# A two-block transformer kernel: in its last mixer, window scores and their softmax are placed between the two compressions

## The reference

```python
def compress(t, pos, w1, w2):
    blocks = t[:, cidx] + pos[None, None, :, None, :]
    flat = blocks.transpose(0, 3, 1, 2, 4).reshape(Bn, G, n_cmp, CMP_BLOCK * E)
    return (jax.nn.gelu(flat @ w1) @ w2).astype(f32)
...
p_c = masked_softmax(q . k_cmp + bias, dist_c >= 0);   o_c = p_c . v_cmp
p_s = masked_softmax(q . k_sel + bias, dist_s >= 0);   o_s = p_s . v_sel
p_w = masked_softmax(q . k_win + bias, valid_w);       o_w = p_w . v_win
out = g[0] * o_c + g[1] * o_s + g[2] * o_w
```

## Time and profile before

| | us |
|---|---|
| median of 3 runs | 2382.18 (2381.37 to 2387.04) |
| the profiled execution | 2387.23 |
| its span (first to last instruction) | 2385.4 |
| PE busy | 2247.4 |
| DVE busy | 1490.9 |
| ACT busy | 1084.2 |

### The profile page before, as it was taken

How to read it: one execution, slowest core, us unless ns; L and a number is a source line. 1 busy time by engine, 2 the same in 40 slices (tenths; PEclk the granted TensorE clock), 3 DMA queues, 4 the chain that set the end, 5 groups by cost and what they waited for, 6 DMA issues and landing times.

```text
span 2385.4 us, 36673 instructions
## 1 busy us (share of the span) xinstructions
PE 2247.4 (94%) x13862; PEld 1876.2 (79%) x13862; DVE 1490.9 (63%) x2345; ACT 1084.2 (45%) x1544; POOL 241.2 (10%) x241
## 2 busy tenths in 40 slices
PE   8999999999999999899999789999989788999997
PEld 6678667999767866799976679887879477988786
DVE  2946355755394635585534677888764267788876
ACT  1132452344214245244433355676654265667665
POOL 1914000101091400021100000000000000000000
PEclk9999899999999999999999989999999898999999
DMA  4332113455333212356532236888845413688884
GB/s 153 127 121 89 63 64 131 165 180 172 121 132 115 88 64 71 136 174 196 187 130 98 71 140 211 314 298 310 294 165 177 141 45 142 221 309 305 303 293 140
DMA packets 109808, 396.86 MB, mean 166 GB/s; under 512 B 12088, under 2 KB 14144, under 8 KB 109376
## 3 DMA queue, kind: packets, MB, share of 16 engines
q1 hardware_dynamic: 108576, 393.45, 48.5%
q10 hardware_dynamic: 1056, 1.06, 0.1%
HBM read 393.40 MB, written 1.06 MB: 165 GB/s over the span
## 4 chain that ended last, share of the span: by engine, by line
PE 80%; DVE 14%; ACT 4%; issue 2%; DMA 1%; DVEq 0%; SPq 0%; ACTq 0%
PE psum L541 78%; DVE W_LO L1642 3%; PE psum L549 1%; DVE region L1647 1%; DMA ring<-in_weights 1%; DVE region L1650 1%; ACT region L1218 1%; DVE RS L1679 1%; DVE X_LO L1647 1%; DVE SQ L1647 1%; ACT W_HI L1213 1%; ACT SQ L1218 0%; ACT L1218 0%; DMA PAR<-in_params 0%; ACT XT L1218 0%
## 5 line engine op out<-in xcount | busy, mean ns | idle before, releaser
L1642 DVE TENSOR_TENSOR W_LO<-ring,W_HI 128x1024 fp32r<-128x1024 f32 x434 | 531.9, 1226 | 217.6 <-ACT W_HI L1213 207.1
L1213 ACT ACTIVATE W_HI<-ring 128x1024 fp32r<-128x1024 f32 x434 | 461.1, 1062 | 330.4 <-PE psum L541 245.3
L541 PE MATMUL psum<-HN,ring 128*128 128x272 f32 (+1 forms) x1600 | 384.3, 401 | 9.7 <-DVE HN L1654 9.7
L541 PEld LDWEIGHTS psum<-HN,ring 128*128 128x128 f32 x1600 | 308.6, 195 | 78.8 <-issue 18.3
L541 PE MATMUL psum<-X_HI,W_HI 128*128 128x256 f32 x800 | 229.1, 286 | 9.3 <-DVE W_LO L1642 6.9
L541 PE MATMUL psum<-X_LO,W_HI 128*128 128x256 f32 x800 | 224.5, 281 | 0.0
L541 PE MATMUL psum<-X_HI,W_LO 128*128 128x256 f32 x800 | 224.4, 280 | 0.0
L1222 ACT ACTIVATE region<-psum 128x272 f32<-128x272 f32 (+9 forms) x227 | 89.7, 395 | 287.2 <-PE psum L541 270.8
L1642 DVE TENSOR_TENSOR W_LO<-SQ,W_HI 128x1024 fp32r<-128x1024 f32 x128 | 156.9, 1226 | 37.1 <-ACT W_HI L1213 32.8
L541 PE MATMUL psum<-FN_HI,W_HI 128*128 128x272 f32 (+1 forms) x592 | 169.2, 286 | 0.0
L541 PE MATMUL psum<-W_HI,XG_HI 128*128 128x512 f32 x384 | 152.9, 398 | 17.3 <-DVE W_LO L1642 15.3
(11 more groups left out here) (323 smaller groups left out, 4268.4 us busy)
## 6 DMA issues: line engine op xcount, KB each, us to landing
ring<-in_weights SPq DMA_DIRECT2D x615, 512.0 KB, 4.2
SQ<-in_weights SPq DMA_DIRECT2D x128, 512.0 KB, 4.8
XT<-in_x SPq DMA_DIRECT2D x1, 1088.0 KB, 5.1
CST<-in_consts SPq DMA_DIRECT2D x1, 1082.5 KB, 7.3
SQ<-bias_by_distance ACTq DMA_DIRECT2D x1, 1024.0 KB, 5.8
out<-XT SPq DMA_DIRECT2D x8, 128.0 KB, 1.9
PAR<-in_params SPq DMA_DIRECT2D x1, 572.0 KB, 8.2
bias_by_distance<-MIX ACTq DMA_DIRECT2D x1, 12.0 KB
```

The lines of the kernel that those rows point to most:

```text
L541: ins = nc.tensor.matmul(dst, w, x, start=start, stop=stop, skip_group_check=True)
L1213: lane(nc.scalar.activation(W_HI[:, s % SPLIT, :], ring_slot(n), ACT.Copy), split_hi)
L1642: lane(nc.vector.tensor_tensor(W_LO[:, s % SPLIT, :], ring_slot(n), W_HI[:, s % SPLIT, :].bitcast(F32), ALU.subtract), split_lo)
```

## The change

`BLK` becomes two tiles, the second in the first 960 columns of `MIX`; `blocks(1)` moves ahead of `compress(0)` and no longer waits for PE. The scores, exponentials and scalings of a head can now be done in two parts: the two token branches ("windows") and the compressed one. The windows of heads 0 and 1 are scored between the two compressions and scaled during the second; behind it come the window scores of head 2 and the transposes of heads 0 and 1, then `compress2`, then the compressed parts of heads 0 to 2. From `c_norm(2)` on the order is that of before. ACT gets two one-element operations, one that loads the GELU table before the second GELU and one that loads the Exp table behind it. The splits for `y_out` are held back to the end of `c_norm_compressed(0)`. Semaphore counts are adapted.

```diff
-        BLK = at_region(960).rearrange("p (i n) -> p i n", i=32)
+        BLK = [b.rearrange("p (i n) -> p i n", i=32) for b in (at_region(960), MIX[:, :, :].rearrange("p k t -> p (k t)")[:, :960])]
...
             def c_scores(h):
+                c_windows(h)
+                c_compressed(h)
+
+            def c_windows(h):
...
+            def c_compressed(h):
+                g = h // 4
+                if h == 0:
+                    for key in (("c_cmp", 0, 0), ("c_cmp", 1, 1)):
+                        banks.await_read(pe, key)
                 dst, done = take("c_c", h)
...
             def compress(s):
+                if s:
+                    fn(RS[:1, T : T + 1], cst("eps", 0, 1, 1), ACT.Gelu_apprx_tanh)
                 src = wait_bank("c_hidden", s)
                 fn(CHID[:30, 2 * s, :], src[:30, :256], ACT.Gelu_apprx_tanh, sem("c_gelu"))
+                if s:
+                    fn(RS[:1, T : T + 1], cst("eps", 0, 1, 1), ACT.Exp)
...
+            def c_windows(h):
+                if h < 2:
+                    c_exps(h, h + 1, (1, 2))
+
+            def c_compressed(h):
+                c_exps(h, h + 4, (0,) if h < 2 else (1, 2, 0))
...
-                follow.paused = name in ("blocks", "compress", "compress2")
-                if name == "c_scores" and args == [0]:
-                    follow(("step", "compress2"))
+                follow.paused = name in ("blocks", "compress", "compress2", "c_windows", "c_compressed", "c_norm_windows", "c_turn_windows")
...
-                if s:
-                    wait_bank("c_hidden", 0)
...
+            def c_norm_windows(h):
+                c_scale(h, 4 * h + 4, (1, 2))
+
+            def c_norm_compressed(h):
+                c_scale(h, 10 + 2 * h, (0,))
...
-            s += [("split_x", 1), ("c_in",), ("blocks", 0), ("compress", 0), ("blocks", 1), ("compress", 1), ("compress2",), ("c_scores", 0), ("c_scores", 1)]
+            s += [("split_x", 1), ("c_in",), ("blocks", 0), ("blocks", 1), ("compress", 0), ("c_windows", 0), ("c_windows", 1)]
+            s += [("c_norm_windows", 0), ("c_norm_windows", 1), ("compress", 1), ("c_windows", 2), ("c_turn_windows", 0), ("c_turn_windows", 1), ("compress2",)]
+            s += [("c_compressed", h) for h in range(3)]
             for h in range(HEADS):
-                s += [("c_norm", h), ("c_turn", h)]
-                s += [("c_scores", h + 2)] if h + 2 < HEADS else []
+                s += [("c_norm_compressed", h), ("c_turn_compressed", h)] if h < 2 else [("c_norm", h), ("c_turn", h)]
+                s += [("c_scores", h + 2)] if 1 <= h < HEADS - 2 else []
                 s += [("c_values", h)] + ([("c_split", h - 2)] if h >= 2 else [])
```

More of the change, by code:

```diff
@@ L1130, in compress @@
                         n = 4 * c + j
-                        mm(dst[:30, :256], BLK[:, n, :], w[:, 256 * j : 256 * j + 256], n == 0, n == 31, done if n == 31 else None)
+                        mm(dst[:30, :256], BLK[s][:, n, :], w[:, 256 * j : 256 * j + 256], n == 0, n == 31, done if n == 31 else None)
             def compress2():
@@ L1151, in c_scores @@
             def c_scores(h):
+                c_windows(h)
+                c_compressed(h)
+            def c_windows(h):
                 g = h // 4
                 if h == 0:
-                    for key in (("c_q", 7), ("c_k", 3), ("c_cmp", 0, 0), ("c_cmp", 1, 1)):
+                    for key in (("c_q", 7), ("c_k", 3)):
                         banks.await_read(pe, key)
@@ L1165, in c_turn, with c_turn_windows, c_turn_compressed @@
             def c_turn(h):
+                c_turn_windows(h)
+                c_turn_compressed(h)
+            def c_turn_windows(h):
                 for b in range(2):
-                    turn_probs(("c_turned", h, b), "c_probs", 3 * h + b + 1, P[2 * (h % 3) + b])
-                pe.wait_ge(sem("c_probs"), 3 * h + 3)
+                    turn_probs(("c_turned", h, b), "c_probs", (2 if h < 2 else 3) * h + b + 1, P[2 * (h % 3) + b])
+            def c_turn_compressed(h):
+                pe.wait_ge(sem("c_probs"), 5 + h if h < 2 else 3 * h + 3)
                 dst, done = take("c_turned", h, 2)
@@ L1606, in c_scores, with c_exps @@
             def c_scores(h):
-                act.wait_ge(sem("c_max"), h + 1)
+                c_exps(h, h + 4, range(3))
+            def c_windows(h):
[3 more added lines that the diff above has]
+                c_exps(h, h + 4, (0,) if h < 2 else (1, 2, 0))
+            def c_exps(h, maxima, branches):
+                act.wait_ge(sem("c_max"), maxima)
                 s = 64 + 20 * (h % 3)
-                for b in range(3):
+                for b in branches:
                     for i in range(2):
@@ L2269, in blocks @@
                         pv = pos[:, 32 * s + 16 * a : 32 * s + 16 * a + 16, None]
[L2270 removed]
+                        tt(BLK[s][:, 16 * a : 16 * a + 16, 15 * g : 15 * g + 15], x[:, :, a : a + 15], bc(pv, [128, 16, 15]), ALU.add,
                            sem("blocks") if (g, a) == (1, 1) else None)
@@ L2281, in c_scores, with c_windows @@
             def c_scores(h):
+                c_windows(h, False)
+                c_compressed(h, False)
+                c_negated(h, 0, 6)
+            def c_windows(h, alone=True):
                 s = 64 + 20 * (h % 3)
@@ L2292, in c_scores, with c_compressed @@
                         free(ins, "c", h, i, b)
+                if alone:
+                    c_negated(h, 2, 4)
+            def c_compressed(h, alone=True):
+                s = 64 + 20 * (h % 3)
                 src = wait_bank("c_c", h)
```

21 lines of the change are left out of this document (14 added, 7 removed).

## The result

| | before | after |
|---|---|---|
| median, runs of the first comparison | 2386.23 (2381.37 to 2392.58, 6 runs) | 2371.5 (2370.1 to 2375.78, 6 runs) |
| ratio, 95% interval | | 0.9947 (0.9932 to 0.9961) |
| the profiled execution, its span | 2387.23, 2385.4 | 2371.86, 2370.1 |
| second comparison, other chip | 2384.8 | 2374.66, ratio 0.9955 (0.994 to 0.9971) |
| third comparison | 2382.46 | 2375.49, ratio 0.9969 (0.9952 to 0.9987) |

The change is faster in all three comparisons. Its 24 runs have a mean of 2374.6 us, the 106 of the kernel before 2383.2: 8.6 us apart, where 8.9 were forecast. Two more executions of the kernel before, with a far lower granted clock (2854.68 us at 0.738 and 3739.7 us at 0.553), are left out.

The account below looks back on a forecast made before the run. PE, busy 94% of the span, bounds the kernel, so gains must come where it idles or is slow. Head 2's scaling moves from 1912.6 to 1903.7, 8.9 us, giving 2378.2, carried to the median 2373.2 us; range 2369 to 2379.

Parts of the forecast that it names:

- The sum: From the first compression's end to head 2's scaling on DVE: 1912.6 - 1903.7 = 8.9 us saved.
- Closing the hole: PE's 4.43 us between the compressions filled by window scores; second compression ends at 1881.1, not 1884.77: 3.6 us saved.
- rival A: Second compression and head loop: late weights and half clock cost 5.8 us at most, gain 3 to 7; chance 0.22.
- Hiding the windows: Window passes, exponentials and scalings of two heads run behind the second compression, ending 1876.4, with 4.7 us to spare.
- The table loads: Four loads on ACT instead of two, each 1.28 us with no time between load and next operation.
- The splits: Output projection's two weight splits stay on the path, only moved; DVE waits about 3.7 us at its first.
- ACT's order at the transposes: Before the compression's second layer, four transpose evacuations stand ahead on ACT, which sets the pace by about 1 us.
- The clock at head 3's scores: Between head 1's and head 2's scalings, half clock assumed: 4.85 us; full clock, 3.09, would gain 1.8 more.
- The loop: From head 2's scaling on, both kernels have the same order; no gain or loss was counted there.
- slower heads: Sign of being wrong: the head loop's heads follow each other more slowly than before.
- Rival B: Head loop: clock stays at 1.2 GHz, costing 12.3 us against 9, so 2385.5, slower; chance 0.03.
- The number itself: Whole kernel: 2378.2 us by the profiled execution's time, carried to the median 2373.2.

Follow-up runs that it names:

- change_2: The changed kernel once more, no edit, on one chip with the two reordered versions, against the kernel before: 2375.49 us (12 runs), ratio 0.9969.
- again: The changed kernel once more, no edit, five rounds, against the kernel before: 2374.66 us, ratio 0.9955.

## Why the prediction was right

**The sum.** 8.9 us were predicted from E to head 2's scaling; the first profile of the change has 8.6 (48.45 against 39.84), the two others 7.7 and 7.8, and the kernel against itself has 0.02 (48.45 and 48.43). Step by step, in us after E:

| step | predicted | first profile |
|---|---|---|
| second compression ends | 16.7 | 16.9 |
| windows of heads 0 and 1 scaled | 12.0 | 11.8 |
| GELU load done | 11.3 | 11.3 |
| compressed scores start | 23.7 | 24.0 |
| head 0's compressed part scaled | 27.1 | 27.7 |
| exponentials of head 2 done | 29.7 | 30.2 |
| DVE waits at its first split | 3.7 long | 3.75 long |
| splits done | 33.3 | 33.9 |
| head 1's compressed part scaled | 34.4 | 35.1 |
| head 2's scaling starts | 39.3 | 39.6 |

**Closing the hole.** Right: 14.10 us for the second compression at a clock of 1.00, where 14.15 were taken. The two terms of that were each a little off. For 32 matmuls the prediction had 13.65, but its own price of 0.43 gives 13.8; what is above that, 0.3, goes with three short waits of the weight loads (0.16 to 0.40), where 0.5 was put. That the weights could be late was a real danger (rival A): with nothing between the two compressions PE waited 1.59 us for them.

**Hiding the windows.** Right: 5 us were to spare, and the added GELU load lies inside them.

**The table loads.** Right: the sum went by 1.28 us with nothing behind. Of the four loads in the rows above each takes 1.28, and for the three whose next operation is shown it starts 0.01 to 0.02 us after the load's end. The Trainium skill (ScalarE: Activation LUTs, section What ACT_TABLE_LOAD costs) has about 1.28 us for the load as well, but a drain of about 1.38 on top of it, 2.66 in all. The trace agrees with it on the load and shows no drain.

**The splits.** Right, and the best supported step: the predicted 3.7 us is the row of 3.75, and taking both splits away (3.75 of waiting, 2.48 of work) brought 4.6 us at head 2's scaling against the first profile of the change, 5.5 against the two others.

**ACT's order at the transposes.** About right: ACT was said to set the pace by about 1 us. At the second layer's products PE waits 1.33 us for ACT in the change (the row at 1878.19), and before it waited 0.54 at that place, so 0.8 us are ACT's:

```profile
1885.55 0.63 PE L541 MATMUL psum<-region,ring 128*128 128x30 f32 x4 [0.54 <-ACT region L1222]
```

What the prediction did not ask is whether the twelve transposes had to stand there at all. Moving them and their evacuations behind the compressed scores brought 2.1 us at equal clock, twice what it put on ACT's order at most.

**The clock at head 3's scores.** Taken as half. Right in the main: the clock was 0.50 up to 1892, and the products there took 5.36 us, between the 5.98 of the half clock and the 3.85 of the full one. The rows have 4.55 us from head 1's scaling (1891.53 + 0.50) to head 2's (1896.58), where 4.85 was taken.

**The loop.** This step did not hold. The prediction gave it nothing, on the ground that its order is the same, and named slower heads as a sign of being wrong. It gave back 1.4 us: of 8.6 us at head 2's scaling 7.2 are left at `y_out` (84.34 against 77.16). From head 2's scaling to `y_out` the three profiles of the change have 36.9 to 37.3 us, the two of the kernel before 35.8 and 35.9. The clock fell twice in each of the three (at the scores of heads 5 and 7, in rows of 5.03 to 5.52 us in place of 3.85) and once in each of the two (5.00 and 5.21). Rival B had the right mechanism in a weak form. The clock came back (1.00 between 1899 and 1905), so its price of 12.3 us never arose. That price was itself too low: it took 2.65 us for the values and transposes of each of the last two heads, where rows of the kernel before have 3.4 for the last (2.17, 0.88 and 0.38). The Trainium skill (TensorE: Matmul & The Clock Gate, section What's actually happening) has the throttled state as the default, which activity releases; these stages agree, with 0.50 where PE had 4.09 us of work in 7 and 1.00 again in the loop. Why the change has one drop more stays open: the profile with the splits moved had none.

**The number itself.** 2373.2 was forecast; 2371.5 came in the first comparison, 2374.3 as the median of all 24 runs. The profiles differ by 15.3 us: 7.2 from E to `y_out`, 0.7 behind it, and 7.4 ahead of E, where PE has the same instructions in both kernels. The last part is not the change's, and in the second profile of the change it had the other sign (5.5 us later than before). The time fell where the prediction said, and its centre was met within 2 us either way. That it was met so closely is partly luck: the stretch to `y_out` is 6.4 to 7.2 us shorter in the three profiles, not 8.9, and the scatter made up the difference. What stays open is whether the change also lets the chip grant a little more clock as a whole: the mean over its runs is 0.9687, over those of before 0.967 to 0.968. By the slope below that would be some 2 us, and these runs don't settle it.

## What to carry to other kernels

When two dense stretches are joined, ask what supplies the second: here the closed hole came back as a wait of 1.59 us for weights, until 2.75 us of other work stood between. When a wait of one engine on another is predicted to be only moved, move its cause as well: with the two splits, the order of the first heads and the twelve transposes moved, the kernel gained nearly as much again as by the whole change (7.4 us over 12 runs). And where the time scatters by more than the effect, compare stretches by their distance from a common instruction, not spans.

## What the runs showed of the hardware

I had not expected one core to scatter this much by its clock. The mean granted clock of a run and its span go together: the twelve runs of change_2 have 2363.1 us at 0.973 and 2378.2 to 2379.1 at 0.966, about 2.2 us for each 0.001. In the profiles E lies between 1849.2 and 1869.9 us for the same instructions. The unchanged part shows it, here from 600 to 1200 us in the first profile of the change and then in that of again (columns as above; the clock is the third number from the end). In the first 300 us PE is busy just as long, but has 1729 records of products in place of 1755:

```profile
600.00:900.00 300.00, 287.37 (x1755) 219.29 (x1754) 162.57 (x220) 88.49 (x134) 94.58 (x78) 0.98 0.29 104
900.00:1200.00 300.00, 289.77 (x2080) 263.15 (x2078) 187.87 (x357) 122.47 (x190) 22.65 (x33) 0.98 0.46 154
```

```profile
600.00:900.00 300.00, 287.38 (x1729) 219.63 (x1728) 157.18 (x208) 87.77 (x133) 94.70 (x78) 0.95 0.30 101
900.00:1200.00 300.00, 292.03 (x2080) 264.50 (x2079) 186.56 (x350) 122.27 (x191) 23.92 (x32) 0.97 0.47 153
```

The same happens inside the stretch: the compressed scores took 1.81 us in the first profile of the change and 2.71 in change_2, by where the half clock began. So about 1 us of two stretches' difference can be the clock's. Where less is claimed above, it rests on the rows of the operations themselves.
